# Low halves, squares and sums around the five norms of a three-block network

## The reference

```
for layer in (0, 1):
    x = x + attention(rms_norm(x, g_mix[layer])) @ w_out[layer]     # site "n" (0 or 1)
    x = x + conv_gated_mlp(rms_norm(x, g_ffn[layer]))               # site "f"
x = rms_norm(x, g_final)                                            # site "g"
h = rmsnorm(x, norm1)                                               # site ("n", 2), then the third block
x = x + gated(h) @ w_out_2
h = rmsnorm(x, norm2)                                               # site ("f", 2), then the expert layer
rms_norm(x, g) = x * rsqrt(mean(x*x, axis=-1) + 1e-6) * g
```

## Time and profile before

| what | value |
|---|---|
| median of 3 runs | 1963.02 us |
| the profiled execution, its own time | 1962.71 us |
| its span | 1960.6 us |
| TensorE busy | 1785.2 us (91%) |
| VectorE, ScalarE, GpSimd busy | 65%, 44%, 40% |
| chain of waits, share by engine | TensorE 64%, VectorE 24%, ScalarE 4%, issue 4%, GpSimd 3% |
| mean granted clock of TensorE | 0.925 |

### The profile page before, as it was taken

How to read it: one execution, slowest core, us unless ns; L and a number is a source line. 1 busy time by engine, 2 the same in 40 slices (tenths; PEclk the granted TensorE clock), 3 DMA queues, 4 the chain that set the end, 5 groups by cost and what they waited for, 6 DMA issues and landing times.

```text
span 1960.6 us, 27291 instructions
## 1 busy us (share of the span) xinstructions
PE 1785.2 (91%) x10680; PEld 1555.1 (79%) x10680; DVE 1281.3 (65%) x2470; ACT 868.9 (44%) x1500; POOL 779.2 (40%) x410
## 2 busy tenths in 40 slices
PE   5999899789989997688889899789999999999997
PEld 4677899677669996555667799789999988888886
DVE  6653674954546758687763459998999944444444
ACT  5443565335336652412432344444444445555553
POOL 3211468432125683175633359770000014444443
PEclk9887899899789998788967899899999999999998
DMA  6421455444115554322321535454444456666664
GB/s 219 140 76 33 167 179 192 145 175 133 54 36 201 181 175 161 132 76 76 105 77 54 179 127 182 149 166 142 144 141 141 149 170 193 194 195 193 194 192 141
DMA packets 77311, 283.19 MB, mean 144 GB/s; under 512 B 8704, under 2 KB 8960, under 8 KB 76800
## 3 DMA queue, kind: packets, MB, share of 16 engines
q1 hardware_dynamic: 75888, 275.97, 43.3%
q10 hardware_dynamic: 1296, 5.49, 0.7%
HBM read 279.33 MB, written 2.10 MB: 144 GB/s over the span
## 4 chain that ended last, share of the span: by engine, by line
PE 64%; DVE 24%; ACT 4%; issue 4%; POOL 3%; DMA 1%; POOLq 0%; DVEq 0%; ACTq 0%
PE bank L468 52%; PE bank L459 9%; DVE wl L1121 4%; DVE tab L1127 2%; DVE H L1127 2%; ACT wh L845 2%; PE bank L551 2%; DVE att L1132 2%; DVE ssb L1127 1%; DVE att L1138 1%; DVE H L1586 1%; DVE H L1592 1%; DVE H L1588 1%; DVE H L1584 1%; DVE H L1590 1%
## 5 line engine op out<-in xcount | busy, mean ns | idle before, releaser
L1709 POOL TENSOR_TENSOR wl<-raw,wh 128x1024 fp32r<-128x1024 f32 x231 | 598.9, 2602 | 862.3 <-ACT wh L845 862.1
L845 ACT ACTIVATE wh<-raw 128x1024 fp32r<-128x1024 f32 x515 | 531.4, 1048 | 175.4 <-PE bank L468 166.0
L468 PE MATMUL bank<-hh,wh 128*128 128x256 f32 x1904 | 545.6, 287 | 18.6 <-DVE hl L1127 17.3
L468 PE MATMUL bank<-hl,wh 128*128 128x256 f32 x1904 | 538.1, 283 | 0.0
L468 PE MATMUL bank<-hh,wl 128*128 128x256 f32 x1904 | 536.8, 282 | 0.0
L1121 DVE TENSOR_TENSOR wl<-raw,wh 128x1024 fp32r<-128x1024 f32 x284 | 402.7, 1426 | 131.0 <-ACT wh L845 130.8
L468 PEld LDWEIGHTS bank<-hh,wh 128*128 128x128 f32 x1904 | 364.4, 191 | 20.9 <-issue 14.4
L468 PEld LDWEIGHTS bank<-hl,wh 128*128 128x128 f32 x1904 | 364.3, 191 | 0.0
L468 PEld LDWEIGHTS bank<-hh,wl 128*128 128x128 f32 x1904 | 363.8, 191 | 0.0
L1127 DVE TENSOR_TENSOR acl<-H,ach 128x256 fp32r<-128x256 f32 x128 | 87.6, 685 | 183.2 <-ACT ach L848 183.2
L468 PE MATMUL bank<-wh,ach 128*128 128x512 f32 x512 | 200.0, 391 | 1.9 <-DVE acl L1127 1.9
(11 more groups left out here) (183 smaller groups left out, 2439.5 us busy)
## 6 DMA issues: line engine op xcount, KB each, us to landing
raw<-in_ut_dram SPq DMA_DIRECT2D x128, 512.0 KB, 3.5
raw<-in_vt_dram SPq DMA_DIRECT2D x128, 512.0 KB, 3.6
raw<-in_wup_dram SPq DMA_DIRECT2D x88, 512.0 KB, 4.0
raw<-in_win_dram SPq DMA_DIRECT2D x48, 512.0 KB, 4.5
raw<-in_wdown_dram SPq DMA_DIRECT2D x44, 512.0 KB, 3.6
raw<-in_wout_dram SPq DMA_DIRECT2D x24, 512.0 KB, 3.5
raw<-in_wga_dram SPq DMA_DIRECT2D x16, 512.0 KB, 3.6
raw<-in_wpq_dram SPq DMA_DIRECT2D x16, 512.0 KB, 3.6
```

The costliest lines, as they stand in the source:

```text
L468: m = p.e.matmul(out, lhs[i][a], rhs[i][b], start=start and i == 0 and j == 0, stop=stop and i == n - 1 and j == 2)
L845: a.e.activation(high_of(u), raw_of(u), ACTF.Copy).then_inc(act_hi.up(("hi", u)), 1)
L1709: g.e.tensor_tensor(low_of(u), raw_of(u), high_of(u).bitcast(F32), ALU.subtract).then_inc(pool_lo.up(("lo", u)), 1)
```

## The change

1. `lower`: the first four units after each of the five sites are all "p", made by GpSimd. Before, by the rows of the stages, GpSimd made one or two of the four.
2. VectorE at the "f" sites (`to_norm`): x's last half (t = 1) is added behind the scaling of t = 0, and nothing is streamed between the scaling and the making of `hl`. Its fourth unit and the row's stream call come last.
3. ScalarE squares halves of 512 (`half_squares`), with a scale of 1/32 in place of VectorE's factor 1/1024, each half as soon as it is added; VectorE adds the two sums and epsilon in one instruction. `hh` of t = 0 is made ahead of the last two units' high halves.
4. GpSimd at the "f" sites: unit 0, root of t = 0, units 1 and 2, root of t = 1, then a wait until VectorE has scaled t = 1, then unit 3. At ("n", 1) and "g": root, then a wait for the scaled result, then the units.
5. The two norms after layer 1: VectorE forms x times the row of "g" in `mix` while ScalarE squares x, and ScalarE then squares that product. The second mean is the product's mean square times the square of the first root, and one multiplication by both roots and the second row gives the outcome, in `hn2`. x itself is rebuilt behind the transposes' low halves, as `mix` times the first root.

The parts stand here in this order: the list `lower`; VectorE's, GpSimd's and ScalarE's program at an "f" site; GpSimd's loop over the down product; VectorE's two norms after layer 1, and what follows them.

```diff
+        normed = [first["wup", L] for L in range(DEPTH)] + [first["win", 1], first["wu"], first["wpq"]]
+            elif any(u <= i < u + 4 for u in normed):
+                lower.append("p")
...
+            def to_norm(st, tag, first_u, row, buf, ev):
...
+                for h in range(3):
+                    if h == 0:
+                        added(1, 0)
+                    if h == 2:
+                        mean(st, 0)
+                        scale(st, 0, buf, row)
+                    stream(first_u + 4 + h)
+                added(1, 1)
+                turned(st, (0,), 2)
+                mean(st, 1)
+                scale(st, 1, buf, row)
+                turned(st, (1,), 2)
+                stream(first_u + 7)
+                stream(row)
...
+            def stream_to_norm(st, first_u, row):
+                stream(first_u)
+                root(st, 0)
+                stream(first_u + 1)
+                stream(first_u + 2)
+                root(st, 1)
+                g.wait_ge(dve_out, ("nrm", st, 1))
+                stream(first_u + 3)
+                stream(row)
...
+            def stream_to_norm(st, first_u, row, buf, ev):
+                for h in range(4):
+                    if h == 0:
+                        half_squares(st, 0, buf, 0, dve_out, ev + (0, 0))
+                        half_squares(st, 1, buf, 0, dve_out, ev + (1, 0))
+                        half_squares(st, 0, buf, 1, dve_out, ev + (0, 1))
+                    if h == 3:
+                        half_squares(st, 1, buf, 1, dve_out, ev + (1, 1))
+                        turned(st, (0,), 2)
+                    stream(first_u + h)
...
                 for f, t in down_order:
-                    if t:
-                        stream(first["wdown", L] + f)
                     if f == NTILE - 1:
                         if L:
                             root("g", t)
                             root(("n", 2), t)
+                            g.wait_ge(dve_out, ("nrm", ("n", 2), t))
                         else:
                             root(("n", 1), t)
+                            g.wait_ge(dve_out, ("nrm", ("n", 1), t))
+                    if t:
+                        stream(first["wdown", L] + f)
...
                         if L:
-                            v.e.scalar_tensor_tensor(x[:, t, :], x[:, t, :], rstd[:, t:t + 1], raw_of(row), ALU.mult, ALU.mult
-                                                     ).then_inc(dve_out.up(("gx", t), ("used", row) if t else None), 1)
-                            norm_scale(("n", 2), t, mix, first["row", "n", 2])
+                            v.e.tensor_tensor(mix[:, t, :], x[:, t, :], raw_of(row), ALU.mult)
+                            mean("g", t, False)
+                            v.wait_ge(pool_out, ("rs", "g", t))
+                            tt(sqg[:, t:t + 1], rstg[:, t:t + 1], rstg[:, t:t + 1], ALU.mult)
+                            v.wait_ge(act_out, ("sq", "g", t, 1))
+                            ts(ms[:, t:t + 1], ss[:, 2 * t + 1:2 * t + 2], sqg[:, t:t + 1], EPS, ALU.mult, ALU.add, ("ms", ("n", 2), t))
+                            v.wait_ge(pool_out, ("rs", ("n", 2), t))
+                            tt(sqg[:, t:t + 1], rstg[:, t:t + 1], rstd[:, t:t + 1], ALU.mult)
+                            v.e.scalar_tensor_tensor(hn2[:, t, :], mix[:, t, :], sqg[:, t:t + 1], raw_of(row2), ALU.mult, ALU.mult)
...
+            turned(("n", 2), (0, 1), 2)
+            for t in range(2):
+                ts(x[:, t, :], mix[:, t, :], rstg[:, t:t + 1], None, ALU.mult, None)
             stream(first["row", "n", 2])
```

More of the change, by code:

```diff
@@ L875, in act @@
             for t in range(2):
-                squares(("n", 0), t, mix, x_in, "x")
+                squares(("n", 0), t, x[:, t, :], mix[:, t, :], 0, x_in, "x")
             turned(("n", 0), (0, 1), 2)
@@ L917, in act @@
                 turned(("m", L), (1,), 2)
[L918 to L926, removed]
+                for h in range(4):
+                    stream(first["wout", L] + h)
+                stream_to_norm(("f", L), first["wout", L] + 4, first["row", "f", L], mix, ("xa", L))
                 if L:
@@ L1044, in act @@
             turned("me", (0, 1), 2)
[L1045 to L1053, removed]
+            for h in range(4):
+                stream(first["wout2"] + h)
+            stream_to_norm(("f", 2), first["wout2"] + 4, first["row", "f", 2], gates[:, :, 1024:2048], ("xa", 2))
             a.wait_ge(dve_out, ("nrm", ("f", 2), 1))
@@ L1296, in add_to_x, with added @@
                 tt(x[:, t, n * 512:(n + 1) * 512], x[:, t, n * 512:(n + 1) * 512], bank[:, :], ALU.add, ev, alone=True)
+            def to_norm(st, tag, first_u, row, buf, ev):
+                def added(n, t):
+                    v.wait_ge(pe_out, ("mm", tag, n, t))
+                    add_to_x(n, t, ps(tag, n, t), ev + (t, n))
+                for h in range(4):
+                    if h in (0, 3):
+                        added(0, h // 3)
+                    stream(first_u + h)
+                for h in range(3):
[9 more added lines that the diff above has]
+                scale(st, 1, buf, row)
+                turned(st, (1,), 2)
+                stream(first_u + 7)
+                stream(row)
             for t in range(2):
-                norm_scale(("n", 0), t, mix, first["row", "n", 0])
+                mean(("n", 0), t, False)
+                scale(("n", 0), t, mix, first["row", "n", 0])
             turned(("n", 0), (0, 1), 2)
@@ L1381, in dve @@
                 turned(("m", L), (1,), 2)
[L1382 to L1392, removed]
+                to_norm(("f", L), ("wout", L), first["wout", L], first["row", "f", L], mix, ("xa", L))
                 for f in range(NTILE):
@@ L1756, in pool @@
                     att_step(c)
-                for n in range(2):
-                    for h in range(4):
-                        if n and h in (0, 3):
-                            root(("f", L), h // 3)
-                        stream(first["wout", L] + 4 * n + h)
-                stream(first["row", "f", L])
+                for h in range(4):
+                    stream(first["wout", L] + h)
+                stream_to_norm(("f", L), first["wout", L] + 4, first["row", "f", L])
                 def y_low(f):
@@ L1820, in pool @@
                 stream(first["wau"] + i)
-            for n in range(2):
-                for h in range(4):
-                    if n and h in (0, 3):
-                        root(("f", 2), h // 3)
-                    stream(first["wout2"] + 4 * n + h)
-            stream(first["row", "f", 2])
+            for h in range(4):
+                stream(first["wout2"] + h)
+            stream_to_norm(("f", 2), first["wout2"] + 4, first["row", "f", 2])
             for c in range(16):
```

76 lines of the change are left out of this document (39 added, 37 removed).

## The result

The changed kernel takes 1939.51 us, the median of four runs (1935.89 to 1941.87); the kernel before, on the same chip, 1962.85 (four runs, 1952.07 to 1963.16). The ratio is 0.9898, with a 95% interval of 0.9859 to 0.9937. I had said 1948.0, 1943.0 to 1954.5: the sign is right and the size is wrong, by 8.5 us. The ratios in this document are formed from the runs within 1.5% of the fastest of their kernel and are not the quotient of the two medians. The profiled execution took 1938.5 and spans 24.1 us less than the one before.

A forecast was written before the change was run, and what follows sets the result against it. It took TensorE, busy nine tenths of the time, as the bound, with only its standstills around five norm sites to shorten. 3 x 1.7 + 2.2 + 7.7 = 15.0 us off 1962.71 gave 1947.7, forecast as 1948.0, range 1943.0 to 1954.5.

The forecast's parts named there:

- The base: Whole kernel: the gain was subtracted from the profiled execution's 1962.71 us, said to stand 0.3 below the median of runs.
- Rival (c): At restarts after the norm sites: shorter pauses keep TensorE's clock up, 4 to 6 us more gained, 1943; chance 10%.
- The "f" sites, 1.7 each forecast: Three "f" sites: VectorE's low halves leave the path, TensorE restarts at 205.1 against 206.78; 1.7 us each, 5.1 in all.
- wins the port, as its wait ends first: "f" sites: the scaling of t = 0 goes ahead of GpSimd's next low half, takes 1.28 us and ends at 195.9.
- a sign of being wrong: Listed as showing the forecast wrong: a GpSimd low half started before a scaling that waits; no size given.
- ("n", 1), 2.2 forecast: Site ("n", 1): VectorE's two low halves go, but TensorE waits for GpSimd's unit 3; gain 2.2 us, between 1.3 and 2.6.
- 1.3, if the stall leaves a low clock: Site ("n", 1): lower end of the gain, 1.3 us in place of 2.2, if TensorE's stall leaves a low clock.
- The two norms, 7.7 forecast: Two norms after layer 1: scaling ends at 802.0, TensorE restarts at 804.6 against 812.27; gain 7.7 us.
- I let each gain through to the end: Behind every site: nothing hangs on a fixed time, so the full 15.0 us reaches the kernel's time.
- (a): All sites: low halves stay on the path, on slower GpSimd; 13 us more than forecast by its sum, 1976; chance 5%.
- (b): Norm sites: GpSimd shuts out every VectorE instruction, additions and `hl` too; 1958.3 us; chance 7%.
- (d): Later stages: the gain is swallowed by a stage another engine bounds from a fixed point, as by loads; 1962.7; chance 4%.

The follow-up runs named there:

- scaling first: Changed kernel, but at the "f" sites GpSimd waits for the scaling of t = 0 before any low half; median 1941.31 us, ratio 0.9797.
- without pauses: Changed kernel without GpSimd's four waits for a scaling; median 1938.59 us over 7 runs, ratio 0.9916.

## Why the prediction was wrong

**The base.** The step that failed first is the one that looks like bookkeeping: "The profiled execution took 1962.71 ... it stood 0.3 below the median of the runs". The profiled execution had drawn the low clock in layer 0's attention, and all three runs lie in the slower group; half of 64 later ones do not. The change moves nothing there, and the four of the changed kernel happened to draw the other side. By the two base values, 1962.7 and the 1951 of the faster group, my own sum gives 1947.7 or 1936; the range had no term for it. The miss of 8.5 us is thus two errors of opposite sign: a base some 12 us too high, and a gain put at 15.0 that the stretches give as 11.5. That 1951 less 11.5 meets the measured 1939.5 so closely is luck, since the runs of one group spread over several us. Rival (c) had the clock in it, but only behind the restarts that the change shortens. The profile of before had the row (0.50 at 132.00 to 150.00), and I did not ask what it would cost if it were 1.00. Shown: the draw, at 15.7 us in that stage; two groups of whole runs, some 11 us apart for the kernel before and 16 for the changed one; and that wide matmuls beside it take it away in all but one or two of 18 runs. Open: what decides it in an execution, and why the groups of the kernel before lie closer together. The two traces do differ further ahead: in 20 to 40 us the granted clock was 1.00 before and 0.87 after, and TensorE's matmuls lie up to 1.28 us apart there. From 63 to 131 us they differ by less than 0.1. The start behind the pause of 1.68 us doesn't decide it either: 128.94 with scaling first, which went low, and 128.97 without pauses, which stayed in full.

**The "f" sites, 1.7 each forecast, 0.6 to 0.8 measured.** The step that failed: "The scaling of t = 0 ... wins the port, as its wait ends first". A GpSimd low half started before a scaling that waits is also what I had named as a sign of being wrong. VectorE and GpSimd of the changed kernel at ("f", 0):

```profile
173.47 0.69 DVE L1139 TENSOR_TENSOR xs<-xs,bank 128x512 f32<-128x512 f32 x1 [4.91 <-PE bank L474]
...
178.89 3.35 DVE L1176 SCALAR_TENSOR_TENSOR mix<-xs,sta,raw 128x1024 f32<-128x1024 f32 x1 [3.73 <-POOL sta L1748]
182.17 0.68 DVE L1139 TENSOR_TENSOR xs<-xs,bank 128x512 f32<-128x512 f32 x1
...
185.66 0.21 DVE L1146 TENSOR_SCALAR sta<-sta 128x1 f32<-128x1 f32 x1
186.55 1.29 DVE L1176 SCALAR_TENSOR_TENSOR mix<-xs,sta,raw 128x1024 f32<-128x1024 f32 x1 [0.67 <-POOL sta L1748]
```

```profile
175.94 2.41 POOL L1743 TENSOR_TENSOR wl<-raw,wh 128x1024 fp32r<-128x1024 f32 x1 [7.27 <-ACT wh L851]
178.31 0.55 POOL L1748 TENSOR_TENSOR sta<-sta 128x1 f32<-128x1 f32 x1
178.82 5.65 POOL L1743 TENSOR_TENSOR wl<-raw,wh 128x1024 fp32r<-128x1024 f32 x2
185.96 0.56 POOL L1748 TENSOR_TENSOR sta<-sta 128x1 f32<-128x1 f32 x1 [1.48 <-DVE sta L1146]
```

The root releases VectorE, but GpSimd's next low half has no wait left: its high half was long there. It starts at 178.82, the scaling 0.07 later, and the scaling takes 3.35 in place of 1.28. The Trainium skill has a sentence on this (SBUF — State Buffer, Who interferes with whom): "Issue order, not op shape, decides who blocks." The trace agrees, by 0.07 us; I had used the section's rule on which instructions contend and not this one. Then the second error follows. I had the root of t = 1 wait for GpSimd; in the trace it waits for VectorE (1.48 us idle ahead of 185.96), as VectorE's order puts `hl` of t = 0 (to 185.63) ahead of the mean of t = 1. The kernel with the scaling of t = 0 first shows the collision at its price (15.2, 1.6 to 1.8 less). The one with both scalings first takes 3.8 less again (11.46), but by two edits at once: units 1 and 2 leave GpSimd's way to the root of t = 1, and the mean of t = 1 no longer waits for `hl`. How the 3.8 divide between them was not measured.

**("n", 1), 2.2 forecast, 1.73 measured.** The mechanism is as described; the term that was too small is the one behind the last quarter. GpSimd's timeline:

```profile
391.30 7.09 POOL L1743 TENSOR_TENSOR wl<-raw,wh 128x1024 fp32r<-128x1024 f32 x3 [1.40 <-DVE mix L1176]
398.35 0.55 POOL L1748 TENSOR_TENSOR sta<-sta 128x1 f32<-128x1 f32 x1
400.29 4.68 POOL L1743 TENSOR_TENSOR wl<-raw,wh 128x1024 fp32r<-128x1024 f32 x2 [1.40 <-DVE mix L1176]
```

The chain of waits (start, us, what):

```profile
402.69 1.94 PE bank L474 x6
404.63 0.87 PE bank L490 x4
...
406.89 1.22 PE bank L474 x2
```

TensorE waits for unit 3 (2.57 us; for unit 2 it waits too, 0.33), runs the last quarter in 1.94 (forecast 1.95), and restarts 4.20 behind the start of that quarter; I had 3.80. The transpositions took 0.87 us where I had 0.45: the granted clock was 0.50 in 404.40 to 406.90, as the forecast had allowed for ("1.3, if the stall leaves a low clock") but not taken. Without pauses, and with both scalings first, the wait for unit 3 was only 1.17 and 1.30 us, and the restart came 3.51 behind.

**The two norms, 7.7 forecast, 7.52 measured.** Restart 17.98 us behind the start of the additions; the forecast was 17.8. VectorE, and GpSimd after the dots:

```profile
769.06 1.39 DVE L1139 TENSOR_TENSOR xs<-xs,bank 128x512 f32<-128x512 f32 x2 [8.10 <-PE bank L474]
...
776.70 2.29 DVE L1448 TENSOR_TENSOR mix<-xs,raw 128x1024 f32<-128x1024 f32 x1
783.08 1.29 DVE L1459 SCALAR_TENSOR_TENSOR att<-mix,sta,raw 128x1024 f32<-128x1024 f32 x1
787.78 2.69 DVE L1144 TENSOR_SCALAR xs<-mix,sta 128x1024 f32<-128x1024 f32 x2
...
775.55 5.66 POOL L1743 TENSOR_TENSOR wl<-raw,wh 128x1024 fp32r<-128x1024 f32 x2 [1.66 <-DVE att L1459]
```

The product of t = 1 is blocked by one unit, as said, and the rebuilding of x lies behind the restart, hidden. The unit that had landed at 807.35 before no longer holds ScalarE: it waits 0.41 us there, and `hh` follows in time.

**The rest.** Half squares took 0.63 (taken: 0.60). The changed scale is worth nothing, as costed. "I let each gain through to the end" can't be confirmed from one pair of traces, since the stages between the sites differ from execution to execution: from the restart behind the two norms to the start of the last addition of t = 0 at ("f", 2) it took 275.6, 277.6, 268.6, 269.9 and 272.1 us in five traces whose kernels share its code (the changed kernel twice, scaling first, no pauses, extra matmuls). The two kernels with extra matmuls let 10.1 of 11.1 through. Of the rivals, (a) and (b) are out (additions and `hl` took 0.67 to 0.69 beside GpSimd). (d) is out too, as that pair shows. (c) as I put it didn't occur: the clock in the "f" stretches is 0.74 and 0.80, where it was 0.79 and 0.78.

## What to carry to other kernels

Before a forecast takes one profile and three runs as its base, look for stretches at a granted clock of 0.50 in which TensorE is busy throughout, and price the other level: here that was larger than the change. When one engine's result releases two others, or itself, write down which of them has no wait left; here it took the port, and a pause on GpSimd is best put where a short instruction on VectorE's critical path would otherwise meet a 2.4 us unit. Compare stretches around the edit, not only whole times, and check whether the order of work on the engine that you freed now delays the next step.

## What the runs showed of the hardware

- The same code, two courses: the attention of layer 0 at 2.4 GHz or at 1.2, 15.7 us apart, and in the two traces compared nothing differs by over 0.1 us in the 68 us ahead. Of the nine traces without extra matmuls four had layer 0 low and five in full. Layer 1 does not follow it: it was low in eight of the nine, after a full layer 0 too, and in full after a low one in the kernel with both scalings first. Eighteen more matmuls of 512 columns made the kernel before 14 us *faster* than itself on the same chip (1952.32 to 1937.97).
- A VectorE instruction with one input in SBUF can be shut out too: TENSOR_SCALAR on 512 values, 0.43 us alone, took 2.51 beside GpSimd's units; with two inputs it was 2.78 against 0.69; moving work to the idle GpSimd slowed the VectorE work that the stage was waiting for.
- When both want the port in turn, GpSimd's unit and a VectorE instruction alternate; the scaling that started 0.07 us behind GpSimd's unit took 2.07 us longer (3.35 in place of 1.28).
